# Gate and up projections by Strassen's seven products, with weight sums on GpSimd

## What is computed

```
def swiglu(x, w_gate_up, w_down):
    g, u = jnp.split(x @ w_gate_up, 2, axis=-1)
    return (jax.nn.silu(g) * u) @ w_down
...
        f = swiglu(rms_norm(h, ffn_norm_pre[layer]), ffn_w_gate_up[layer], ffn_w_down[layer])
        h = h + rms_norm(f, ffn_norm_post[layer])
...
        ff = (jax.nn.silu(hn @ w_gate) * (hn @ w_up)) @ w_down
        h = h + rms_norm_2(ff, ffn_post_g)
```

## Time and profile before

| what | value |
|---|---|
| three timed runs | 2074.09, 2074.70, 2077.65 us; median 2074.7 |
| profiled execution, span from first to last instruction | 2073.7 us |
| TensorE, VectorE, ScalarE, GpSimd busy | 99, 56, 34, 0% |
| chain that ended last | TensorE 94%, VectorE 3%, ScalarE 2% |
| granted TensorE clock | 0.998 of full speed |

### The profile page before, as it was taken

The page is one execution under the profiler, slowest core; times in us unless marked ns, Lnnn a source line. Parts: engine busy times, 40 slices in busy tenths (PEclk is TensorE's granted clock), DMA queues, the critical chain, the costliest instruction groups (busy, mean ns, idle before and its releaser), DMA issues.

```text
span 2073.7 us, 26061 instructions
## 1 busy us (share of the span) xinstructions
PE 2054.0 (99%) x10234; PEld 1717.1 (83%) x10234; DVE 1164.8 (56%) x1960; ACT 707.1 (34%) x1088; POOL 9.7 (0%) x23
## 2 busy tenths in 40 slices
PE   9999999999999999999999999999999999999998
PEld 8888888888889898898887888888888678888887
DVE  6647444432784766757758744441398975444323
ACT  4225322221522323333235422221344663222213
POOL 0000000000000000000000000000000000000000
PEclk9999999999999999999999999999999999999999
DMA  5862222222225142151332122222222122222221
GB/s 191 107 113 79 102 101 101 84 105 95 82 101 143 62 119 85 61 143 62 107 98 82 61 98 88 98 101 101 101 103 82 41 102 82 101 101 88 100 96 61
DMA packets 37193, 198.53 MB, mean 96 GB/s; under 512 B 3911, under 2 KB 7016, under 8 KB 15736
## 3 DMA queue, kind: packets, MB, share of 16 engines
q1 hardware_dynamic: 29008, 181.48, 25.0%
q10 hardware_dynamic: 7176, 13.23, 2.9%
q0 software_dynamic: 928, 2.70, 2.6%
HBM read 181.14 MB, written 3.67 MB: 89 GB/s over the span
## 4 chain that ended last, share of the span: by engine, by line
PE 94%; DVE 3%; ACT 2%; issue 1%; DMA 0%; DVEq 0%; POOL 0%; SPq 0%; ACTq 0%; POOLq 0%
PE bank L1699 80%; PE bank L1742 5%; PE bank L2030 2%; PE bank L1988 2%; PE bank L2006 1%; DVE c L1514 1%; PE bank L1731 1%; DVE work L1009 1%; PE bank L2175 0%; PE bank L2047 0%; PE bank L2200 0%; DVE work L1074 0%; ACT w_hi L557 0%; DVE h L1077 0%; PE bank L2274 0%
## 5 line engine op out<-in xcount | busy, mean ns | idle before, releaser
L1699 PE MATMUL bank<-x_hi,w_hi 128*128 128x512 f32 x1568 | 620.5, 396 | 0.0
L1699 PE MATMUL bank<-x_hi,w_lo 128*128 128x512 f32 x1568 | 611.0, 390 | 0.0
L1699 PE MATMUL bank<-x_lo,w_hi 128*128 128x512 f32 x1568 | 610.4, 389 | 0.0
L970 DVE TENSOR_TENSOR w_lo<-w_raw,w_hi 128x2048 fp32r<-128x2048 f32 (+1 forms) x149 | 301.7, 2032 | 422.2 <-ACT w_hi L557 422.1
L557 ACT ACTIVATE w_hi<-w_raw 128x2048 fp32r<-128x2048 f32 (+1 forms) x132 | 249.9, 1894 | 356.0 <-PE bank L1699 327.1
L1699 PEld LDWEIGHTS bank<-x_hi,w_hi 128*128 128x128 f32 x1568 | 294.4, 188 | 65.7 <-issue 5.8
L1699 PEld LDWEIGHTS bank<-x_hi,w_lo 128*128 128x128 f32 x1568 | 294.3, 188 | 62.4
L1699 PEld LDWEIGHTS bank<-x_lo,w_hi 128*128 128x128 f32 x1568 | 294.6, 188 | 60.1 <-issue 1.2
L1699 PE MATMUL bank<-ff_hi,w_hi 128*128 (+2 forms) x542 | 208.1, 384 | 0.0
L1699 PE MATMUL bank<-ff_lo,w_hi 128*128 (+2 forms) x542 | 207.9, 384 | 0.0
L1699 PE MATMUL bank<-ff_hi,w_lo 128*128 (+2 forms) x542 | 207.9, 384 | 0.0
(11 more groups left out here) (224 smaller groups left out, 2272.3 us busy)
## 6 DMA issues: line engine op xcount, KB each, us to landing
w_raw<-w_all SPq DMA_DIRECT2D x167, 1024.0 KB, 4.9
qk<-qk_next ACTq DMA_DIRECT2D x32, 384.0 KB, 10.7
w_raw<-w_all SPq DMA_DIRECT2D x6, 256.0 KB, 6.9
h<-x_t SPq DMA_DIRECT2D x3, 512.0 KB, 8.0
skew<-erow POOLq DMA_DIRECT2D x8, 192.0 KB, 8.7
out_t<-h SPq DMA_DIRECT2D x3, 512.0 KB, 3.0
bias<-skew POOLq DMA_DIRECT2D x8, 128.0 KB, 6.3
w_raw<-w_all SPq DMA_DIRECT2D x4, 128.0 KB, 3.8
```

Of the source, the lines that this page charges most:

```text
L970: ins = v.tensor_tensor(w_lo[p][:, part], raw, hi, ALU.subtract)
L1699: ins = mm(out, b if flip else a, a if flip else b, start=start and n == 0, stop=stop and n == 2, **kw)
```

## The change

The first four gate/up units of each stage stay as they were (`PLAIN = 4`); the 18 others become **form units**. The 2 x 2 product of quarters (inputs in two halves, output blocks in two, tokens in two halves) is made with seven products for eight, in Winograd's form. The quarters lie in a unit in the order of `quarters_unit`; the seven weight forms are B11, B22, B21 (raw quarters) and T1, T2, T3, T4 (sums). A product is four blocks x three matmuls of 256 columns. It needs:

- four sums of activation quarters per stage, made by GpSimd (`x_sums`) from a scaled copy `x_f` of h, rounded by ScalarE and split by VectorE (`forms`);
- per unit three additions on GpSimd (`w_sums`, 1024, 512 and 512 elements per partition), seven roundings of 512 on ScalarE, four splits on VectorE (512, 1536, 1024, 512);
- per unit four intermediate results copied from PSUM by ScalarE (`keep`), and their sums on VectorE (`out_crossed`, `out_main`, `out_side`), which also apply `r_pre`.

The late products B22 and T4 of a unit run behind B11 of the next. To make room, gate times up is stored unsplit (`ff`) and rounded and split in the down stage into a ring of five buffers (`ff_round`, `ff_rest`). The forms of even units lie where h was: h is written to memory (`h_save`) at the start of each gate/up stage and read back in the down stage. The sums `w_sum` lie where `f_lo` is written, so the split of T1 to T3 waits for all three additions.

```diff
+            def x_sums(fi, t, u0):
+                for k in range(KC):
+                    pool.wait_ge(h_ready, blocks_ready(t, k))
+                    nc.gpsimd.tensor_scalar(x_f[:, k, :], h[:, k, :], gain(PRE_GAIN[t] + k), None,
+                                            ALU.mult).then_inc(x_scaled, 1)
...
+                pool.wait_ge(xstat_done, t + 1)
...
+                add(x_sum[0][:], a22, a21, ALU.subtract).then_inc(x_formed, 1)
...
+            def w_sums(fi, u0, l, i=None):
...
+                pool.wait_ge(w_landed[p], run(i, 16, 16 * (u // 2)))
+                if i is None:
+                    pool.wait_ge(unit_done, u0 + 2 + 2 * n)
+                else:
+                    pool.wait_ge(prod_done, run(i, 12, prod_count(fi, n - 2, 3)))
+                add = nc.gpsimd.tensor_tensor
+                both = slice(Q * QT1, Q * QT3 + Q)
+                add(w_sum[f][:, both], w_raw[p][:, 0:2 * Q], w_raw[p][:, Q:3 * Q], ALU.add).then_inc(w_summed, 1)
+                pool.wait_ge(w_summed, run(i, 6, count + 1))
+                add(w_sum[f][:, quarter(QT2)], w_sum[f][:, quarter(QT1)], w_raw[p][:, quarter(RAW_OF[QB22])],
+                    ALU.add).then_inc(w_summed, 1)
...
+                def window(l, i=None):
+                    first_quarter(l + 1, i)
+                    keep(l, 0, i)
+                    summed_quarters(l + 1, i)
+                    keep(l, 1, i)
+                    late_quarter(l + 1, QB22, i)
+                    keep(l, 2, i)
+                    late_quarter(l + 1, QT4, i)
+                    keep(l, 3, i)
+                    if l % 2:
+                        act.wait_ge(out_scaled, run(i, 2, (FORM_UNITS // 2) * fi + (l - PLAIN + 1) // 2))
+                        silu((l - 1) // 2, i)
...
+                act.dma_start(h_save.rearrange("m p s -> p m s"), h[:]).then_inc(h_saved, 16)
...
+            def ff_round(fi, c):
+                act.wait_ge(ff_made, 11 * fi + c + 1)
+                nc.scalar.activation(ring_hi[ring_of(c)][:].rearrange("p a s -> p (a s)"), ff[:, c, :],
+                                     ACT.Copy).then_inc(ffhi_done, 1)
...
+                def window(l, i=None):
+                    out_crossed(l - 1, i)
+                    split_quarters(l + 1, 0, i)
+                    out_main(l - 1, i)
+                    split_quarters(l + 1, 1, i)
+                    out_side(l - 1, i)
+                    split_quarters(l + 1, 2, i)
+                    split_quarters(l + 1, 3, i)
...
+                def form_product(l, q):
...
+                    for k in range(4):
+                        at = slice(Q * q + P * k, Q * q + P * k + P)
+                        for n, (wt, x) in enumerate(((f_hi[f], hi), (f_hi[f], lo), (f_lo[f], hi))):
+                            ins = mm(out, wt[:, at], x[:, k, :], start=q in (QB11, QT3, QB21) and k == 0 and n == 0,
+                                     stop=k == 3 and n == 2, skip_group_check=True)
...
+                def form_unit(l, i=None):
+                    n = l - PLAIN
+                    pe.wait_ge(evac, run(i, 4, ev + l - 1))
+                    split_wait(l, 1, i)
+                    form_product(l, QB11).then_inc(prod_done, 1)
+                    if n:
+                        late_products(l - 1, i)
+                    split_wait(l, 2, i)
+                    pe.wait_ge(part_kept, kept_count(fi, n, 0, i))
+                    form_product(l, QT2).then_inc(prod_done, 1)
+                    form_product(l, QT3).then_inc(prod_done, 1)
+                    pe.wait_ge(part_kept, kept_count(fi, n, 1, i))
+                    form_product(l, QT1).then_inc(prod_done, 1)
+                    split_wait(l, 3, i)
+                    form_product(l, QB21).then_inc(prod_done, 1)
```

More of the change, by code:

```diff
@@ L710, in _ @@
             pre_norm(1)
-            ffn(FFN_A, EV_FFN_A, 0, 0)
-            down(DOWN_A)
+            ffn(0, 1, FFN_A, EV_FFN_A)
+            down(0, DOWN_A)
             post_norm(2)
@@ L1816, in rows @@
+            def rows(u, c, hi, lo, start=False, i=None, per=2, taken={}, banks=range(KC), base=None):
+                pe.wait_ge(w_split, run(i, per, u + 1))
                 for kk in range(2):
-                    n = 2 * c + kk if i is None else 2 * 2 * i + (2 * c + kk)
+                    n = (2 * c if base is None else base) + kk
                     for m in banks:
```

443 lines of the change are left out of this document (340 added, 103 removed).

## The result

The changed kernel takes 2106.3 us (median of four runs, 2103.9 to 2107.8) for 2075.2 before: 1.0145 times as long, 95% interval 1.0131 to 1.0160 (the two medians alone give 1.0150). The prediction was 2036 us. Its rival (a), engines that take turns at the memory, had put 2103.

What follows compares the result with a forecast made beforehand. TensorE, busy 99% of the span, bounds the kernel; 54 units x 0.82 us save 44.2, less 5 for pauses at the stages' ends, so 39 off the 2074.7 us median: 2036 us, range 2031 to 2120 (own range 2031 to 2048).

Steps and rivals of the forecast that it cites:

- rival (a): GpSimd adds and VectorE operations with two SBUF inputs exclude each other: 11.0 us per unit, 2103 us; chance 0.41.
- All of the above lets them read memory together: Forecast's assumption for VectorE and GpSimd on long operations at once; no trace row for or against.
- every engine fits in 10.06 us: Per changed unit: VectorE 6.9 us, ScalarE 5.4, GpSimd 4.6, each set against TensorE's 10.06.
- I keep the clock there: TensorE's clock stays at its upper level, 2.4 GHz, its longest pause being under 1 us.
- Half-length matmuls at 0.120 us: TensorE in changed units: 84 matmuls of 256 columns at 0.1198 us, 10.06 us, saving 0.82 per unit.
- Fifth unit's second product: Start of the changed units: T2 waits 0.62 us for a copy, no late products standing before it.
- Down stage: At its start the first split of activations comes 0.8 us late.
- seam: Rival (a)'s term between stages: VectorE's split of unit three comes late, 2.4 us per stage.
- The save of h: Writing h (2 MB) at the gate/up stage's start: 10 to 12 us, some 5 more beside a weight transfer.
- Rival (c): Changed order gives the gain back, 0.1 us pause at each of eight waits: 2075 to 2079 us; chance 0.06.
- (d): GpSimd far slower, from about 4.3 ns per element, 9.1 us per unit: near 2079 us; chance 0.04.
- sixth unit's start: Rival (a)'s term at the start of the changed units: 4 us more per stage.

Runs made afterwards that it cites:

- reordered kernel: Kernel with all arithmetic off GpSimd (sums on VectorE, activation scaling on ScalarE), ScalarE's and VectorE's order at the stage's start changed: 2044.0 us.
- half-dose run: Second and third weight sum of each unit, 512 elements each, put back on GpSimd in the reordered kernel: 2066.0 us.

## Why the prediction was wrong

*The step that failed* is the sentence "All of the above lets them read memory together". The forecast's check that every engine fits in 10.06 us added up each engine by itself: 6.9 us for VectorE, 4.6 for GpSimd. For the part of both that reads SBUF they are one sum: VectorE's 5.9 us and the 5.1 that GpSimd's adds take undisturbed make 11.0, for 11.15 measured. VectorE's busy time rose by 149.7 us over the kernel without weight sums (1522.0 less 1372.3), 2.8 us a unit, and GpSimd's adds took 6.24 us a unit for 5.14 undisturbed (2.41, 1.36 and 1.37). I saw this as rival (a) with 0.41 against 0.42, since no row of before showed the two engines beside each other; the answer was not in that trace.
The rule on the Trainium skill's page SBUF — State Buffer (Who interferes with whom), which the prediction weighed, is what the runs show for adds: the later of the two waits. By it alone (a) should have been the forecast. The trace adds that the one that waits can wait for more than the operation it met (three of VectorE's, at 324.02).

A second step failed with it: "Since TensorE never stops before or after the change (its longest pause below is under 1 us), I keep the clock there". The fifth unit waited 3.2 us in each stage, and behind each such wait the granted clock was at 0.50 for 3.4 to 6.8 us. This is small in the changed kernel (at most about 1 us a stage), and some 6 us, by the same estimate, where VectorE makes the weight sums.

*Right.* Half-length matmuls at 0.120 us: 0.120 in the changed kernel while the clock is up, and 10.10 us for a unit without disturbance, for 10.06. Fifth unit's second product: 0.62 us forecast, 0.62 measured. Down stage: 0.8 forecast, 0.73. With the adds off the memory, the forecast's sum holds: 2042 and 2044 us for 2036. Of the 6 us, 18 x 3 x 0.04 = 2 are in the unit and some 2.4 in the seam, after which the fifth unit starts 0.8 us later than 96 matmuls of before would end (232.05 for 231.23); the rest I have not placed. The save of h took 13.5 us (10 to 12 forecast, some 5 more beside a weight transfer), and nobody waited for it. Rival (c) fell with the run without sums, (d) with the length of an add that nothing stands against: 2.41 us for 1024 elements, 2.4 ns each for the 4.3 it needed.

*Rival (a), term by term.* Unit 11.0 forecast, 11.15 measured (2.2 us per stage forecast, 4.9 measured); sixth unit's start 4 forecast, instead the fifth unit waits 3.2; seam 2.4 forecast, 1.0 in the first stage; down 0.8 and 0.7. The sum is 9.4 against 10.8. That 2103 lies so near to 2106 is thus in part luck: the units were put 2.7 us a stage too low, the seam 1.4 and the start 0.8 too high. (Its lower end, 10.5 us a unit, comes to 2076 by its own terms and not 2077.)

The fifth unit's wait has the same cause as the rest. While GpSimd forms the activation sums (210.30 to 223.69 us, where the forecast had them done by 218.7), VectorE splits them:

```profile
218.21 12.13 DVE L1328 SCALAR_TENSOR_TENSOR form_lo<-x_sum,form_hi 128x1024 fp32r<-128x1024 f32 x4
...
233.18 2.07 DVE L1343 TENSOR_TENSOR f_lo<-w_raw,f_hi 128x512 fp32r<-128x512 f32 x1 [1.64 <-ACT f_hi L759]
```

These four splits take 12.13 us for 4.62 in the reordered kernel. Only behind them come the results of the third unit, for which ScalarE's silu waits 6.79 us, and the fifth unit's first rounding stands behind that silu. The first split (233.18) then takes 2.07 us beside an add, and TensorE starts at 235.40. GpSimd's scaling of the activations was mis-sized too, 0.53 us for 512 elements by the memset rate and 2.28 measured, but it ends at 206.35 and GpSimd is idle after it.

I counted one step of the mechanism too kindly: not only does VectorE wait for adds, the three sums are a chain, and VectorE stands still for the last of them for 0.86 us a unit. The half-dose run shows that such a wait, at 2.0 us a unit, can cost 22 us (2066.0 for 2044.0) where VectorE's own operations are hardly lengthened.

## What to carry to other kernels

Before moving element-wise work from VectorE to GpSimd, add both engines' times for operations with two inputs in SBUF, as if they were one engine; what VectorE does on PSUM results, and what GpSimd merely writes, lies outside the sum, and one-operand scalings on GpSimd cost far less than adds (8 us for 62). Ask as well who stands still for the moved work: a chain of sums that VectorE waits for costs it time even where nothing is lengthened. The work moved here was cheaper on VectorE itself: 2.6 us a unit, against 6.2 on GpSimd and 2.8 more for VectorE. Where an algorithm lightens the engine that sets the pace, make the first test one with the new side work left out (2042 us here): it says at once whether the idea or its placement is at fault. And where TensorE is to set the pace, price a pause of some 3 us at more than its length: in these kernels the clock was at half speed for 3.4 to 6.8 us behind it.

## What the runs showed of the hardware

- A GpSimd add and a VectorE operation of two SBUF inputs do not run together: the later one waits. An add of 2.41 us became 3.82, and a split of 0.69 became 2.56. The add was passed by VectorE operations issued after it, as long as they followed each other closely. VectorE operations with one input in PSUM kept their 0.41 to 0.43 us in every changed kernel, and memsets disturbed nothing (splits at 690 and 685 ns).
- A one-operand scaling on GpSimd is itself slow, 1.49 us for 512 elements for an add's 1.28 to 1.37, yet disturbs VectorE far less. In the kernel before, a 2048-element split beside it stays at 2291 ns, while four scalings take 7.91 us beside that split and 6.33 in the next unit. The mechanism is not shown. The Trainium skill's page SBUF — State Buffer (Who interferes with whom) makes no difference between GpSimd instructions that read one operand or two; for one operand the measurement decides against it.
- One-input VectorE operations in and out of SBUF on 4-byte elements run at 0.43 us for 512 elements, for 0.69 with two inputs, and also wait for an add (1.18 us). The Trainium skill's page SBUF — State Buffer (Who interferes with whom) lists such operations, when they run in a mode that uses both ports, among those that can take turns with GpSimd; the trace agrees.
- From the end of each wait of 3.2 us (of 2.9 in another kernel) TensorE's granted clock was at 0.50, 1.2 GHz, for 3.4 to 6.8 us, and 256-column matmuls started every 0.21 us for 0.12. Behind the waits of up to 1.5 us in the middle of the stages it stayed up.
